# The FFNs' first tiles: three instead of four of them in halves of 256 tokens, the fourth in one piece

## What is computed

```python
def swiglu(h, w_gate, w_up, w_down):
    return (jax.nn.silu(h @ w_gate) * (h @ w_up)) @ w_down

for i in range(DEPTH):                      # DEPTH = 2, D_MODEL = 1024, D_FF = 2816
    f = swiglu(rmsnorm(x, ffn1_pre_norm[i]), ffn1_w_gate[i], ffn1_w_up[i], ffn1_w_down[i])
    x = x + 0.5 * rmsnorm(f, ffn1_post_norm[i])
    h = rmsnorm(x, mix_pre_norm[i])
    ...                                     # m = the mixer of the layer
    x = x + rmsnorm(m, mix_post_norm[i])
    f = swiglu(rmsnorm(x, ffn2_pre_norm[i]), ffn2_w_gate[i], ffn2_w_up[i], ffn2_w_down[i])
    x = x + 0.5 * rmsnorm(f, ffn2_post_norm[i])
```

## Time and profile before

| | |
|---|---|
| median of 3 runs | 2089.24 us (2089.02 to 2089.79) |
| the profiled execution | 2088.85 us |
| its span, first to last instruction | 2086.8 us |
| PE busy | 2076.9 us |
| DVE busy | 1244.1 us (60%) |
| ACT busy | 864.0 us (41%) |
| HBM traffic | 177 GB/s over the span |
| granted TensorE clock, mean | 0.999 |

### The profile page before, as it was taken

One profiled execution on the slowest core, in us unless ns is written; L12 is line 12 of the kernel. 1 busy time (PEld: TensorE's weight loads), 2 busy tenths in 40 slices (PEclk: granted clock), 3 DMA queues, 4 the chain that ended last, 5 costly groups with the idle time before them and its releaser, 6 DMA issues.

```text
span 2086.8 us, 26124 instructions
## 1 busy us (share of the span) xinstructions
PE 2076.9 (100%) x10362; PEld 1744.5 (84%) x10362; DVE 1244.1 (60%) x1803; ACT 864.0 (41%) x1255; POOL 81.4 (4%) x79
## 2 busy tenths in 40 slices
PE   9999999999999999999999999999999999999998
PEld 8888888888888888988888888888897779888887
DVE  6455577576665644655457854555775647445575
ACT  5222265444555533422236532223654544222263
POOL 0000000000000000000000100000024100000000
PEclk9999999999999999999999999999999999999999
DMA  7667595221221214557568566667743124666594
GB/s 261 216 212 241 192 332 168 90 91 61 61 61 61 72 51 141 192 197 246 192 226 314 180 228 206 212 242 254 261 130 115 51 71 156 208 222 232 193 333 144
DMA packets 144411, 371.28 MB, mean 178 GB/s; under 512 B 10353, under 2 KB 10993, under 8 KB 144290
## 3 DMA queue, kind: packets, MB, share of 16 engines
q1 hardware_dynamic: 83440, 229.14, 34.7%
q10 hardware_dynamic: 60850, 140.47, 17.7%
HBM read 297.22 MB, written 71.30 MB: 177 GB/s over the span
## 4 chain that ended last, share of the span: by engine, by line
PE 96%; DVE 2%; DMA 1%; ACT 1%; issue 0%; POOL 0%; DVEq 0%; ACTq 0%; SPq 0%; POOLq 0%
PE ps L1166 18%; PE ps L1167 18%; PE ps L1168 18%; PE ps L1174 10%; PE ps L1176 10%; PE ps L1175 10%; PE ps L1479 1%; PE ps L1193 1%; DVE w_lo L1813 1%; PE ps L1698 1%; PE ps L1727 1%; PE ps L1547 1%; DMA raw<-in_w_down 1%; PE ps L1702 1%; PE ps L1403 1%; PE ps L1404 1%
## 5 line engine op out<-in xcount | busy, mean ns | idle before, releaser
L1166 PE MATMUL ps<-h_hi,w_hi 128*128 128x512 f32 (+1 forms) x1832 | 679.5, 371 | 0.2
L1168 PE MATMUL ps<-h_hi,w_lo 128*128 128x512 f32 (+1 forms) x1832 | 674.0, 368 | 0.0
L1167 PE MATMUL ps<-h_lo,w_hi 128*128 128x512 f32 (+1 forms) x1832 | 673.8, 368 | 0.0
L586 ACT ACTIVATE w_hi<-raw 128x1024 fp32r<-128x1024 f32 x432 | 454.4, 1056 | 487.1 <-PE ps L1168 338.6
L1813 DVE TENSOR_TENSOR w_lo<-raw,w_hi 128x1024 fp32r<-128x1024 f32 x417 | 502.2, 1220 | 118.2 <-ACT w_hi L586 116.8
L1166 PEld LDWEIGHTS ps<-h_hi,w_hi 128*128 128x128 f32 x1832 | 345.5, 189 | 58.6 <-issue 1.8
L1168 PEld LDWEIGHTS ps<-h_hi,w_lo 128*128 128x128 f32 x1832 | 345.3, 188 | 57.9
L1167 PEld LDWEIGHTS ps<-h_lo,w_hi 128*128 128x128 f32 x1832 | 345.5, 189 | 55.7 <-issue 0.2
L1813 DVE TENSOR_TENSOR extra<-a_rows,ps 128x512 f32<-128x512 f32 x88 | 60.6, 688 | 408.1 <-PE ps L1168 384.9
L1174 PE MATMUL ps<-w_hi,a_split 128*128 128x512 f32 x616 | 240.3, 390 | 0.6 <-DVE update L1813 0.6
L1176 PE MATMUL ps<-w_hi,a_split 128*128 128x512 f32 x616 | 239.7, 389 | 0.0
(11 more groups left out here) (241 smaller groups left out, 2221.3 us busy)
## 6 DMA issues: line engine op xcount, KB each, us to landing
raw<-in_w_gate_up SPq DMA_DIRECT2D x176, 512.0 KB, 4.5
a_rows<-in_w_down ACTq DMA_DIRECT2D x44, 1024.0 KB, 9.7
sums<-a_rows ACTq DMA_DIRECT2D x44, 1024.0 KB, 7.8
raw<-sums SPq DMA_DIRECT2D x80, 512.0 KB, 5.4
raw<-in_w_down SPq DMA_DIRECT2D x60, 512.0 KB, 4.1
spilled<-extra ACTq DMA_DIRECT2D x44, 512.0 KB, 4.7
normed<-spilled ACTq DMA_DIRECT2D x44, 512.0 KB, 6.2
raw<-in_w_vg SPq DMA_DIRECT2D x16, 512.0 KB, 3.6
```

The costliest lines, as they stand in the source:

```text
L586: return nc.scalar.activation(to, source, ACT.Copy, scale=scale)
L1166: nc.tensor.matmul(to, w_h, hi, start=first, stop=False)
L1167: nc.tensor.matmul(to, w_h, lo, start=False, stop=False)
L1168: return nc.tensor.matmul(to, w_l, hi, start=False, stop=last)
```

## The change

A table `HALVED` gives the number of tiles that `first_four` does in halves: 3 in FFNs, 4 in the mixers. `ffn` starts its loop over full-width tiles with tile 3, and there waits for `update1_done`, which `first_four` had waited for in half 0. Nothing outside PE's program is touched.

```diff
+HALVED = [3 if s in FFN_OF else 4 for s in range(N_SUB)]
...
                 for half in range(2):
                     pe.wait_ge(h_lo_ready, 8 * s + 4 * half + 4)
-                    for m in range(2 if (s, half) == (0, 0) else 0, 4):
+                    for m in range(2 if (s, half) == (0, 0) else 0, HALVED[s]):
                         if half == 0:
                             slot_ready(first + m)
                             if s:
...
             def ffn(f, s):
                 first = first_slot[s]
                 first_four(s)
-                for n in range(4, 2 * FT):
+                for n in range(HALVED[s], 2 * FT):
+                    if n == 3 and s:
+                        pe.wait_ge(update1_done, NC * s)
                     if n >= 8:
                         pe.wait_ge(a_ready, FT * f + (n - 8) // 2 + 1)
                     slot_ready(first + n)
```

## The result

The changed kernel takes 2094.31 us in the median of 20 runs (2092.32 to 2098.48), the kernel before 2089.16 us in the median of 20 (2088.03 to 2091.36). The ratio is 1.0026, 95% interval [1.0019, 1.0032]: 5.2 us slower. Forecast were 2094.7 us and +5.5 us.

A forecast was written before the change was run, and what follows sets the result against it. PE was taken as the bound, busy 2076.9 of 2086.8 us. Stops of 6.6 us less 1.2 us saved, put at +5.5 us on the median 2089.24, gave 2094.7 us; 8-in-10 range 2092.0 to 2097.0.

The forecast's parts named there:

- The lost cover: In four FFNs, PE stops for `h_lo` before half 1 of tile 0, directly behind chunk 3's transposes; 6.6 us in all.
- the 0.3 us for a late `w_lo`: At tile 3's old start in s = 2 and s = 5: a 0.3 us wait inside the new one, bringing nothing.
- The saving of whole tiles: Tile 3 of each FFN in one piece saves 0.29 us, 1.2 over four FFNs (bounds 1.2 and 1.3).
- The page's figure: The Trainium skill's 2.5 ns per matmul beside its columns: tile 3 whole saves 0.06 us per FFN, 0.24 in all.
- The rest of the program at nothing: Outside the stops and tile 3: added `update1_done` wait, earlier `slot_done` and DMAs bring no gain or loss.
- one of my signs of being wrong: In the changed kernel's profile: the forecast is wrong if PE's waits elsewhere shrink by more than 0.5 us.
- The clock: Rival, 6%: PE's clock falls in the stops, the next half tile runs at half speed; 11.5 us more, 2106 us.
- Lateness taken back: Rival, 5%: PE's later waits for `update`, `late_rows`, `normed` and `o_lo` shrink by 2.7 us; 2.8 remain, 2092.0 us.
- the argument against it: At PE's later waits: the releasers, ACT and DVE, work on what PE just made, so are late together with PE.

The follow-up runs named there:

- cover_only: The changed kernel with tile 3 behind the halves made in two pieces of 256 tokens again; 2095.24 us against 2088.83 for the kernel before, ratio 1.0028.
- hi_first: The changed kernel with half 1 of tile 0 starting on `h_hi` products, chunk 3 transposed earlier in s = 0 and 3; 2087.90 and 2087.88 us, ratios 0.9993 and 0.9998.
- split8: The kernel before with tiles 4 to 11 of each FFN made in two pieces of 256 tokens; 2098.11 us against 2088.57, ratio 1.0050.
- halved2: The changed kernel with only two tiles in halves in s = 2, 3 and 5; 2105.94 us against 2088.57 for the kernel before, ratio 1.0083.

## Why the prediction was right

Slower by 5.2 us [1.0019, 1.0032] was measured, 5.5 forecast, by the mechanism that it named.

- **The lost cover** was forecast at 1.81, 1.50, 1.81 and 1.51 us and measured at 1.81, 1.50, 1.82 and 1.51. The three parts of that step each held: the chain from the transposes to `h_lo` kept its 1.26 us, PE went on 0.05 us behind DVE, and the 0.3 us for a late `w_lo` in s = 2 and s = 5 lay inside the new wait. `cover_only` and `hi_first` show the cost alone (+6.4 us) and its end (-0.9 and -0.7).
- **The saving of whole tiles** was taken as 0.29 us each, with 0.32 as the other end; the changed trace gives 11.23 - 10.90 = 0.33, `split8` 0.30 over 32 tiles. The term was 0.04 to 0.16 us too small in all. The page's figure would have given 0.06.
- **The rest of the program at nothing.** This is the weak step. I took every wait of one profile as part of the kernel, and so wrote that no wait of PE hangs on a DMA. The wait for `update` does, over ACT and DVE: it differs by up to 1.6 us from one execution to the next. I had also expected the transposes of chunk 3 in s = 0 at the old time; they came 0.91 us early, by the clock. And one of my signs of being wrong came true in the first profile: the wait for `update` shrank by 0.6 us, more than the 0.5 that I allowed. Neither moves the four stops, but they made the distance of the two first spans 3.5 us where the sum was 5.5. The prediction held nothing for either; that they come out near nothing in the medians of 20 is in part luck.
- **The clock** was a rival at 6%. In the changed kernel it did not fall: the windows over the four stops show 1.00 in all five profiles of the changed kernel and in that of `cover_only`. With longer idleness it does, as `halved2` shows. The price that I set, 2.88 us per FFN, was too high for what it was there, 1.35 and 2.35 us.
- **Lateness taken back** was a rival at 5%, with 2.8 us of loss left. The interval of the 20 runs begins at 1.0019, 4.0 us, so it didn't happen at that size. In part it did, at the wait for `update` in s = 2, and the argument against it, that the releasers are late together with PE, fails there: in the trace of before they wait for the weights' DMAs. With the stops (6.64 us) and the saving (1.2 to 1.3) as measured the sum is 5.3 to 5.4 us, with 5.2 measured; what is taken back is not told apart from that.

Not settled either is why the changed kernel's runs scatter more, 2092.3 to 2098.5 us, where those of before lie between 2088.0 and 2091.4. The profiles show one wait of up to 1.6 us and a start that moves by 1.3 us, which does not reach 6, and the mean clocks of the runs, 0.998 to 1.000 for either kernel, do not set the long ones apart.

## What to carry to other kernels

Work that stands behind a handover (here eight transposes whose result goes through two engines) is cover, and its worth is the length of that chain less what is left in front of the wait, not its own cost: 2.88 us of half tile hid 1.5 to 1.8 us of wait, and merging it saved 0.3. Before instructions are merged or moved, read from the trace when the next consumer's data lands; if they are moved all the same, begin the consumer with the products whose operand lands first. And take waits that come from DMAs from several profiles: one execution shows a value of a spread.

## What the runs showed of the hardware

The granted clock of PE fell in `halved2` behind two stops of 2.02 and 1.68 us with 1.3 us of transposes between them, in s = 2 and in s = 5, and not behind one of 1.57 in the changed kernel, nor behind 1.07 and 1.41 in s = 3. The fall came in the second stop and hit the dense work that followed: in s = 2 1.60 us and some 1.5 of the next 2.00 us ran at 1.2 GHz, in s = 5 about 5.5 us. A stop can thus cost more than its length.

Between the end of DVE's `h_lo` and PE's next matmul lie 0.05 to 0.06 us at each of the 20 stops in the five profiles of the changed kernel.

At the very start the windows' clock misleads. The four matmuls that spread the gain row (timeline of PE) took in before and after

```profile
3.89 3.78 PE L1219 MATMUL ps<-temps,ones 1*128 1x512 f32 x4
```

```profile
3.89 2.05 PE L1220 MATMUL ps<-temps,ones 1*128 1x512 f32 x4
```

though the window from 3.9 to 5.8 us has a granted clock of 1.00 in both. The kept record has its first entry at 12.1 us in before and at 4.1 in after, and the views show 1.00 ahead of it. The matmuls tell the level: they start 0.85 us apart in before and 0.43 in after, and the transposes from 8.6 to 10.3 us in before start 0.21 us apart under a window of 1.00, as they do in after, where the window from 8 to 10 us shows 0.50. Ahead of the first entry the level is to be read from the pace of the matmuls.
